# Value products of an attention block as three split products on divided probabilities, two turns moved by a step, and a last normalisation with scales and biases held in PSUM

## What is computed

```python
h = x @ w_in
qa, ka, va, ga, qb, kb, vb, gb = jnp.split(h, splits, axis=-1)
s = q @ k.T * scale + bias            # masked, per head: 256 x 256
p = jnp.exp(s - s.max(-1)); den = p.sum(-1)
o = (p @ v) / den                     # per head: 256 x 64
y = merge(o) * silu(g)                # 256 x 2048
x = _layer_norm(DEEPNORM_ALPHA * x + y @ w_out, ln_gain, ln_bias)
```

## Time and profile before

| what | value |
|---|---|
| median of 3 runs | 2275.21 us (2274.9 to 2275.25) |
| the profiled execution, its own time | 2275.09 us |
| its span in the profile | 2273.3 us |
| mean granted clock of TensorE | 0.998 |
| PE busy | 2256.3 us, 99% of the span |
| DVE, ACT, POOL busy | 54%, 43%, 9% |

### The profile page before, as it was taken

One profiled execution on the slowest core, in us unless ns is written; L12 is line 12 of the kernel. 1 busy time (PEld: TensorE's weight loads), 2 busy tenths in 40 slices (PEclk: granted clock), 3 DMA queues, 4 the chain that ended last, 5 costly groups with the idle time before them and its releaser, 6 DMA issues.

```text
span 2273.3 us, 24852 instructions
## 1 busy us (share of the span) xinstructions
PE 2256.3 (99%) x10652; PEld 1880.0 (83%) x10652; DVE 1224.4 (54%) x978; ACT 971.7 (43%) x840; POOL 204.0 (9%) x206
## 2 busy tenths in 40 slices
PE   9999999999999999999999999999999999999997
PEld 7888888888888888888888888888888888888886
DVE  5467635545555545555445444554455565665656
ACT  6454554433334443344433333433444444444532
POOL 1003100000000000000100000000100122253201
PEclk9999999999999999999999999999999999999999
DMA  8544456676666666655566556555556755655663
GB/s 274 185 141 156 148 166 206 195 210 205 205 194 203 199 205 207 222 185 185 186 193 196 185 186 198 180 195 189 184 187 206 241 189 171 188 166 183 209 230 111
DMA packets 213533, 435.60 MB, mean 192 GB/s; under 512 B 8596, under 2 KB 9328, under 8 KB 212528
## 3 DMA queue, kind: packets, MB, share of 16 engines
q1 hardware_dynamic: 205600, 408.98, 54.9%
q0 software_dynamic: 7680, 24.98, 4.8%
q10 hardware_dynamic: 144, 0.07, 0.0%
HBM read 421.93 MB, written 12.06 MB: 191 GB/s over the span
## 4 chain that ended last, share of the span: by engine, by line
PE 96%; DVE 2%; ACT 1%; POOL 1%; DMA 1%; issue 0%; SPq 0%; DVEq 0%; POOLq 0%; ACTq 0%
PE acc L1236 30%; PE acc L1237 30%; PE acc L1238 30%; PE side L1246 2%; PE side L1276 1%; PE side L1333 1%; PE side L1320 1%; PE side L1306 1%; DMA bia<-rb_scratch 0%; DVE X L1049 0%; DVE X L1045 0%; POOL DD L558 0%; DMA X<-in_x 0%; DVE wlo L880 0%; DVE cum L1096 0%
## 5 line engine op out<-in xcount | busy, mean ns | idle before, releaser
L880 DVE TENSOR_TENSOR wlo<-raw,whi 128x2048 fp32r<-128x2048 f32 x382 | 893.2, 2338 | 800.5 <-ACT whi L619 800.4
L619 ACT ACTIVATE whi<-raw 128x2048 fp32r<-128x2048 f32 x382 | 731.6, 1915 | 758.2 <-PE acc L1238 758.2
L1236 PE MATMUL acc<-whi,setA_lo 128*128 128x512 f32 x1792 | 701.9, 392 | 0.1
L1237 PE MATMUL acc<-wlo,setA_hi 128*128 128x512 f32 x1792 | 697.8, 389 | 0.0
L1238 PE MATMUL acc<-whi,setA_hi 128*128 128x512 f32 x1792 | 697.7, 389 | 0.0
L1236 PE MATMUL acc<-whi,setB_lo 128*128 128x512 f32 x1280 | 503.5, 393 | 0.0
L1237 PE MATMUL acc<-wlo,setB_hi 128*128 128x512 f32 x1280 | 498.4, 389 | 0.0
L1238 PE MATMUL acc<-whi,setB_hi 128*128 128x512 f32 x1280 | 498.2, 389 | 0.0
L1236 PEld LDWEIGHTS acc<-whi,setA_lo 128*128 128x128 f32 x1792 | 336.8, 188 | 70.2 <-DVE wlo L880 0.9
L1238 PEld LDWEIGHTS acc<-whi,setA_hi 128*128 128x128 f32 x1792 | 336.6, 188 | 70.0
L1237 PEld LDWEIGHTS acc<-wlo,setA_hi 128*128 128x128 f32 x1792 | 336.8, 188 | 68.5
(11 more groups left out here) (191 smaller groups left out, 955.2 us busy)
## 6 DMA issues: line engine op xcount, KB each, us to landing
raw<-in_w_in SPq DMA_DIRECT2D x190, 1024.0 KB, 5.2
raw<-in_w_ffn_up SPq DMA_DIRECT2D x64, 1024.0 KB, 5.3
raw<-in_w_ffn_down SPq DMA_DIRECT2D x64, 1024.0 KB, 5.1
raw<-in_w_gla_out SPq DMA_DIRECT2D x16, 1024.0 KB, 5.0
raw<-in_w_conv_out SPq DMA_DIRECT2D x16, 1024.0 KB, 5.1
raw<-in_w_o SPq DMA_DIRECT2D x16, 1024.0 KB, 5.1
raw<-in_w_out SPq DMA_DIRECT2D x16, 1024.0 KB, 5.1
t_scratch<-t5v POOLq DMA_DIRECT2D x8, 512.0 KB, 7.2
```

What stands on the lines that cost most here:

```text
L619: e.activation(whi[r][:, :, :], raw[r][:, :, :], ACT.Copy).then_inc(s_hi, 1)
L880: e.tensor_tensor(wlo[r][:, :, :], raw[r][:, :, :], asf(whi[r][:, :, :]), ALU.subtract).then_inc(s_lo, 1)
L1236: e.matmul(o, xl, whi[r][:, k, :], start=kk == 0, stop=False)
L1237: e.matmul(o, xh, wlo[r][:, k, :], start=False, stop=False)
```

## The change

**Values.** The operands are swapped: the stationary operand is a block of 64 value columns (one head), and the 256 columns of transposed probabilities are streamed. Values and probabilities are split into fp32r parts (`vhi`, `vlo`, `PT`, `PTl`), so that a head takes three products for each half of the keys: 12 matmuls with 256 streamed columns for two heads, in one PSUM bank. The result comes out transposed and ACT copies it to `YT`. The division moves ahead: the exponential sums its rows on ACT (`accum_out`), and DVE divides `Sm` (`divide`) before the transposition.

**Steps.** Even steps of `att` now have the transposes of two heads and the scores of two heads, odd steps the values of two heads.

**Turns.** `q2` and `y` are turned a step later (at `4u + 5`, an odd step). The gate is turned without a product before it, and DVE multiplies it with `YT` after the turn.

**The end.** The job `bank_ln` copies gains and biases of the columns 0 to 1407 into PSUM banks that are idle by then. DVE takes these columns in pieces of 512, 512 and 384, ACT and POOL take 640 columns in two pieces of 320. There are five output transfers for each half instead of four.

```diff
+         "yb": ("turn_yb",), "wo": ("turn_wo",), "up": ("turn_up",), "q2": ("none", "turn_qk2"),
+         "k2": ("turn_qk2",), "y": ("none", "turn_y")}
...
+    if s in (372, 380):
+        out.append(("bank_ln", s // 8 - 46))
...
     if job == "att":
-        return ([("values", a - 2)] if a >= 2 else []) + ([("probs", a - 1)] if 1 <= a <= 32 else []) \
-            + ([("scores", a), ("scores", a + 1)] if a < 32 and a % 2 == 0 else [])
+        if a % 2:
+            return [("values", (a - 3) // 2)] if a >= 3 else []
+        return ([("probs", a - 2), ("probs", a - 1)] if a >= 2 else []) \
+            + ([("scores", a), ("scores", a + 1)] if a < 32 else [])
...
+        vcols = (slice(0, 512), slice(512, 1024), slice(1024, 1408))
+        pcols = (slice(1408, 1728), slice(1728, 2048))
+        gain_at = (side[0][:, :], side[1][:, :], acc[0][0][:, 0:384])
+        bias_at = (side[2][:, :], side[3][:, :], acc[0][1][:, 0:384])
...
+                    for t in range(2):
+                        e.activation(vhi[j][:, t, :], acc[u % 2][t][:, :], ACT.Copy,
+                                     scale=rstd[2][:, t:t + 1]).then_inc(s_vh, 1)
...
+                            e.wait_ge(*full("values", p))
+                            e.activation(YT[0:64, p, :], side[n % 4][0:64, 0:256], ACT.Copy)
+                            e.activation(YT[64:128, p, :], side[n % 4][0:64, 256:512], ACT.Copy).then_inc(s_read[n % 4], 1)
...
+                                e.activation(Sm[b][:, t, :], Sm[b][:, t, :], ACT.Exp, bias=nmx[b][:, t:t + 1],
+                                             accum_out=den[b][:, t:t + 1]).then_inc(s_ex, 1)
+                    elif job == "bank_ln":
+                        e.wait_ge(s_ln, 32)
...
+                        for i in ((0, 1), (2,))[a]:
+                            e.activation(gain_at[i], lngB[:, vcols[i]], ACT.Copy).then_inc(s_lb, 1)
+                            e.activation(bias_at[i], lnbB[:, vcols[i]], ACT.Copy).then_inc(s_lb, 1)
...
+                    for t in range(2):
+                        e.wait_ge(s_vh, 2 * j + t + 1)
+                        e.scalar_tensor_tensor(out=vlo[j][:, t, :], in0=acc[u % 2][t][:, :], scalar=rstd[2][:, t:t + 1],
+                                               in1=asf(vhi[j][:, t, :]), op0=ALU.mult, op1=ALU.subtract).then_inc(ev, 1)
...
+            def divide(h):
+                b = h % 2
+                e.wait_ge(s_ex, 2 * h + 2)
+                e.reciprocal(rd[b][:, :], den[b][:, :]).then_inc(s_dv, 1)
...
+                for t in range(2):
+                    d = e.tensor_scalar(Sm[b][:, t, :], Sm[b][:, t, :], rd[b][:, t:t + 1], None, ALU.mult)
+                d.then_inc(s_pn, 1)
...
             for s in range(NS):
+                for job, a in jobs(s):
+                    if job == "att" and a < 32 and a % 2:
+                        divide(a - 1)
+                        divide(a)
                 if s + 2 < NS:
                     split(s + 2)
...
+                        for b in range(2):
+                            n = SN["turn", a, b]
+                            k = 4 * j + 2 * b
+                            v = YT[:, k:k + 2, :]
+                            e.wait_ge(*full("turn", a, b))
+                            e.tensor_tensor(v, two(side[n % 4][:, :]), v, ALU.mult).then_inc(s_read[n % 4], 1)
+                            e.wait_ge(s_yh, 2 * j + b + 1)
+                            e.tensor_tensor(A_lo[:, k:k + 2, :], v, asf(A_hi[:, k:k + 2, :]), ALU.subtract).then_inc(s_yl, 1)
...
+                            e.wait_ge(s_ph, h + 1)
+                            e.tensor_tensor(PTl[h // 8][b][:, :, :], two(side[n % 4][:, :]), asf(PT[b][:, :, :]),
+                                            ALU.subtract).then_inc(s_read[n % 4], 1)
...
             def probs(h):
-                e.wait_ge(s_ex, 2 * h + 2)
+                e.wait_ge(s_pn, h + 1)
...
+                for i in range(2):
                     for s in range(2):
-                        f = e.matmul(bank[:, 65 * t:65 * t + 65], PT[b][:, s, 128 * t:128 * t + 128],
-                                     v1[g % 2][:, s, h % 8, :], start=s == 0, stop=s == 1)
+                        for n, (x, y) in enumerate(((vlo[g], PT), (vhi[g], PTl[g]), (vhi[g], PT))):
+                            f = e.matmul(bank[0:64, 256 * i:256 * i + 256],
+                                         x[:, s, 128 * j + 64 * i:128 * j + 64 * i + 64],
+                                         y[i][:, s, :], start=s == 0 and n == 0, stop=s == 1 and n == 2)
```

More of the change, by code:

```diff
@@ L246, in two_block_program @@
         lnbB = at("lnbB", "B", 8 * KB, [128, D])
-        v1 = [at(f"v1{i}", "W", 4160 * i, [128, 2, 8, 65]) for i in range(2)]
+        vhi = [at(f"vhi{g}", "W", 4 * KB * (g % 2), [128, 2, 512], f32r) for g in range(4)]
+        vlo = [at(f"vlo{g}", "A", (16, 20, 16, 24)[g] * KB, [128, 2, 512], f32r) for g in range(4)]
+        PTl = [[at(f"PTl{g}{i}", "A", ((0, 0, 0, 8)[g] + 2 * i) * KB, [128, 2, 256], f32r) for i in range(2)]
+               for g in range(4)]
         wlr = at("wlr", "W", 0, [128, 16, 16])
@@ L265, in two_block_program @@
         nmx = [small(f"nmx{i}", [128, 2]) for i in range(2)]
+        den = [small(f"den{i}", [128, 2]) for i in range(2)]
         rd = [small(f"rd{i}", [128, 2]) for i in range(2)]
@@ L385, in ready @@
             if kind == "out" and j == 0:
-                return seen("turn", UI["y", kk // 4], part % 2)
+                return s_yl, part + 1
             return None
@@ L849, in scalar @@
                             if h >= 2:
-                                e.wait_ge(*full("values", h - 2))
-                            e.activation(PT[b][:, :, :], two(side[n % 4][:, :]), ACT.Copy).then_inc(s_read[n % 4], 1)
+                                e.wait_ge(*full("values", h // 2 - 1))
+                            e.activation(PT[h % 2][:, :, :], two(side[n % 4][:, :]), ACT.Copy).then_inc(s_ph, 1)
                         for h in ((a, a + 1) if a < 32 and a % 2 == 0 else ()):
@@ L866, in scalar @@
                 e.wait_ge(s_nmu, t + 1)
-                e.activation(xv, xv, ACT.Identity, scale=r, bias=m).then_inc(s_oa, 1)
+                for c in pcols:
+                    e.activation(X2[:, t, c], X2[:, t, c], ACT.Identity, scale=r, bias=m).then_inc(s_oa, 1)
         def vector(e):
@@ L1149, in vector @@
                             e.tensor_tensor(B_lo[:, k:k + 2, :], v, asf(B_hi[:, k:k + 2, :]), ALU.subtract).then_inc(s_cv, 1)
-                    elif job in ("turn_yb", "turn_up", "turn_y"):
+                    elif job == "turn_y":
+                        j = UNITS[a][1]
+                        e.wait_ge(*seen("values", 4 * j + 3))
+                        for b in range(2):
+                            n = SN["turn", a, b]
+                            k = 4 * j + 2 * b
+                            v = YT[:, k:k + 2, :]
[3 more added lines that the diff above has]
+                            e.tensor_tensor(A_lo[:, k:k + 2, :], v, asf(A_hi[:, k:k + 2, :]), ALU.subtract).then_inc(s_yl, 1)
+                    elif job in ("turn_yb", "turn_up"):
                         j = UNITS[a][1] % 4
@@ L1423, in tensor @@
                     elif job == "att":
-                        if a >= 2:
-                            values(a - 2)
-                        if 1 <= a <= 32:
-                            probs(a - 1)
-                        if a < 32 and a % 2 == 0:
-                            scores(a)
+                        if a % 2:
+                            if a >= 3:
+                                values((a - 3) // 2)
+                        else:
+                            if a >= 2:
+                                probs(a - 2)
+                                probs(a - 1)
+                            if a < 32:
+                                scores(a)
         block = ctx.enter_context(nc.Block())
```

125 lines of the change are left out of this document (56 added, 69 removed).

## The result

The changed kernel takes **2269.32 us**, the median of 12 runs (2268.7 to 2270.28); the kernel before took 2275.13 (2274.12 to 2276.31), also in 12. The ratio is 0.9975, its interval 0.9966 to 0.9984: **5.8 us faster**, where 7.4 were forecast. The profiled execution took 2269.17 us (before 2275.09) with a span of 2267.3 (before 2273.3).

A forecast was written before the change was run, and what follows sets the result against it. PE was taken to bound the kernel up to its last product. Savings of 5.0 us for 16 pairs, 0.6 for a wait and 1.8 at the end make 7.4 off 2275.09: 2267.7 us, 8-in-10 range 2265.4 to 2271.5.

The forecast's parts named there:

- What bounds the kernel: Until its last product the kernel is the sum of what PE executes; other engines' work is free unless PE waits.
- The even step: Attention's even steps: eight transposes and the scores of two heads take 1.87 us, the slower step behind adds 0.13.
- The odd step: Attention's odd steps: twelve value products at 0.117 us, 1.40 in all (bounds 1.36 and 1.44), next step 0.01 longer.
- The pair: A pair of heads costs 3.41 us above its products instead of 3.72, saving 0.31, or 5.0 us for 16 pairs.
- The turns: The first gate's turn loses its 0.6 us wait for `Y`; three moved q turns cost nothing, within 0.1 us.
- Work that costs nothing: Added DVE and ACT work in attention costs PE nothing: the split ends at 12 us, PE needs it at 16.
- a bias late by 1.4 us fits in: In attention's DVE chain, a bias fetch late by 1.4 us was claimed to cause PE no wait.
- rival B: PE gets a new wait for the division's split or `PTl`: 0.3 us a pair, 4.8 us, 2272.5; chance 0.10.
- rival D: Last stage: PSUM operands don't spare DVE or POOL, 1.6 us less gain, 2269.3; no chance of its own.
- The end: Last normalisation: half 1 starts earlier, PSUM operands spare DVE, POOL is last with 1.07 us per 320 columns; 1.8 us saved.
- Rival A: Value products change the array's mode and pay as scores do, 0.3 us in 16 visits, 4.8 us, 2272.5; chance 0.08.
- Rival C: Weight loads set the pace at the value products, 14.2 us more, 2281.9; decided at 0.155 us a product; chance 0.04.

The follow-up runs named there:

- k: Changed kernel with the gate turn's multiplications first and step 360's splits last, plus 128 stationary columns (both heads) in the value products, half the output rows unused; 2270.01 us.
- a: Changed kernel with the old last normalisation stage and without `bank_ln`; 2271.46 us.
- h: Changed kernel with the splits of step 360 moved behind that step's other jobs, on ACT and DVE; 2268.70 us.
- i: Changed kernel with the gate turn's multiplications first and step 360's splits last, plus only the hi x hi value products, 4 instead of 12 a pair; 2256.01 us.
- c: Changed kernel with its new column pieces, but DVE reads gains and biases from SBUF, without `bank_ln`; 2272.14 us.
- d: Changed kernel with gains and biases in PSUM, but the old columns: three pieces of 512 on DVE, one on ACT and POOL; 2269.26 us.
- f: Kernel before, with only the turns of `q2` and `y` a step later; 2274.46 us.
- b: Kernel before, with only the new last normalisation stage; 2272.84 us.
- g: Changed kernel with both DVE multiplications with `YT` ahead of both subtractions in the turn of `y`; 2267.73 us.

## Why the prediction was right, and where it was off

- **What bounds the kernel.** Right: PE is busy or ready all the way, but for 1.3 us in the rows of its waits behind the first block.
- **The even step.** Right: 1.86 us, forecast 1.87. The slower step behind the scores was put at 0.13 and is 0.17 to 0.18, some 0.7 us in 16 pairs. The kernel before has the same 0.18 at step 317, the one place where scores stand alone (5.62 us), and 0.13 only where values stand ahead of them; the forecast took the 0.13. Why it is so isn't settled.
- **The odd step.** Twelve products at 0.117 were forecast, and they take 0.114, so 1.36 us, the lower bound. I took the price of the 16-column block, but the 64-column block behaves like half of a product of 512 (0.113); the upper bound, the 80*128 rows, was near the price of 128 columns, as k shows (0.119; its visits are 0.07 us longer, which makes the 1.03 us by which its PE's gain, 4.08, is lower). The step behind costs 0.03 and not 0.01. The pair saves 0.29 us, forecast 0.31: 4.6 against 5.0.
- **The turns.** `y0`'s wait went, 0.65 for 0.6. The q turns cost 0.15, where at most 0.1 was allowed.
- **The step that failed: "Work that costs nothing".** The work of DVE and ACT was put at nothing, with 4 us to spare. It cost 1.7 us, and the forecast was 1.6 us better than the result; the smaller terms nearly cancel. The estimate was for the steady pairs, and there it held: no pair between 318 and 356 has a wait. It wasn't made for the places where a second job shares DVE and ACT with a pair: the gate's turn (step 358), whose multiplication now frees a bank that the scores need, and the table load for the gate's SiLU (step 361). Part of it is the sentence that a bias late by 1.4 us fits in: the bias is late just ahead of the gate's turn, 1.82 us in the changed kernel's trace, and where it was earlier (a, h) step 358 has no wait. This is rival B's kind of wait, but in two places and not in each pair. It had 0.10 for 4.8 us.
- **What the number doesn't show.** 2269.32 us lies in the forecast's range, and it is also, to 0.02, what rival D gave, whose mechanism fell. The time alone would have borne out the wrong one; the runs tell them apart.
- **The end.** The forecast of 1.8 us was 2.1 to 2.25 in the medians (2.2 to 2.7 from the last product on in the traces, of which the last transfer's landing moves up to 1.1). Right: half 1 starts when PE is done (8.09 us behind half 0, forecast 8.17), DVE is spared by the operands in PSUM, and POOL is last. DVE took 0.74 for 0.69. The term that was mis-sized is POOL's: 0.86 us for 320 columns instead of 1.07, since I drew a line through 512 and 1024 columns and 320 lies below it. That is 0.8 us in four operations. It was partly given back by the last transfer (0.9 in the profiled execution).
- **Rival A.** The rule of the Trainium skill ("TensorEngine Tiling (Array Packing)", Key Properties), that a change of tiling mode drains TensorE, would have had a drain show at each visit. No row of this case shows one for the 64-column block, neither ahead of the four products of i nor behind the twelve of the changed kernel. For the scores' 64 rows a cost is there (0.2 us in them, and 0.17 in the next step); whether it is a drain no run tried.
- **Rival C** fell: 0.114 us a product is far below 0.155. **Rival D** fell with c and d.

All in all: pairs 4.6, wait 0.65, q turns -0.15, new waits -1.7 and the end 2.1 to 2.25 make 5.5 to 5.7 us, where the medians show 5.8. (The 2.1 is from a run in which one of the waits is missing, so the sum can't be held to better than 1 us.)

## What to carry to other kernels

Where one engine bounds a kernel, "the others have slack" has to be worked out at the worst place, not in the steady state: where a turn, a table load or a bank's release meets the new work. What two single lines of 0.7 us in the wait list stand for took more than a third of what the 16 pairs brought, and a reordering of two instructions gave it back. A run without a wait doesn't show that its edit removed it: look whether the edit stands ahead of the place, and whether an input simply came earlier. When VectorE and GpSimd work at one time, try putting an operand that VectorE would fetch from SBUF into an idle PSUM bank (2.8 us here); how the columns are shared out matters less.

## What the runs showed of the hardware that was not expected

- A product with 256 streamed columns depends on the width of the stationary block, and not in the order one might guess: 0.114 us with 64 columns, 0.117 with 16, 0.119 with 128. With 128 stationary and 64 streamed columns it is 0.108.
- POOL's addition takes 0.86 us for 320 columns, 1.26 for 512 and 1.90 for 1024: no straight line goes through the three.
- The last output transfer lands 2.0 to 3.3 us after its issue (2.02 before, 2.15 in b, 2.83 in the changed kernel, 2.98 in g, 3.10 in a, 3.26 in h), with no link to its size that I could find: a and the kernel before have the same last stage. This stays open, and it is as large as what an edit at the end can bring.
- The start-up differs by some 2.6 us between profiled executions ahead of any change: step 304 starts 0.9 us earlier than before in the changed kernel and 1.7 later in f. Of the 0.9, 0.8 lies in the first six products of 512 columns (9.22 to 11.93 us before, 9.12 to 11.02 with the change). Of the kernel before, then of the changed one:

```profile
10.01 0.63 PE L1237 MATMUL acc<-wlo,setA_hi 128*128 128x512 f32 x1
10.44 0.63 PE L1238 MATMUL acc<-whi,setA_hi 128*128 128x512 f32 x1
```

```profile
9.84 0.40 PE L1289 MATMUL acc<-wlo,setA_hi 128*128 128x512 f32 x1
10.09 0.40 PE L1290 MATMUL acc<-whi,setA_hi 128*128 128x512 f32 x1
```

They follow each other in 0.43 us there and in 0.25 here, on the same work. The trace's record of TensorE's granted clock begins, at full speed, 11.6 us into the kernel before and 9.8 us into the changed one, which is where the distance falls to the usual one in each. For the time ahead of that there is no record, so that TensorE was at its lower clock there is likely (0.43 is nearly twice the usual 0.227), but not shown. In f the first input also came later: the list of PE's waits has 2.9 us for it instead of 1.8.
